# Output projection of the first layer begun inside the last head pair

## The chip, the cores and the metric

The kernel runs on one core of a Trainium2 chip. The metric is the time of one launch in device microseconds (us), as the median of several runs. All times below are microseconds unless marked ns. Engines: PE is the tensor engine (PEld its weight loads), DVE the vector engine, ACT the scalar engine, POOL the GpSimd engine, SP the sync engine, which here issues nearly all DMAs. Each engine runs its instructions in program order.

## The reference, cut to what matters

Two layers of a trunk run over 640 tokens (512 latent tokens and 128 prompt tokens) of width 1024. In the first layer twelve RWKV-7 heads give 768 features and a Fourier mixer gives 256; one output projection joins them, and a mixture of 16 experts follows.

```
h = rmsnorm(x, norm_mix[l]) * (1 + sc1) + sh1
...
o_a, s_fin = rwkv7_mixer(h, r, k, v, ...)      # 12 heads of 64
o_b = fourier_mixer(u)                          # 256 features
mixed = concatenate([o_a, o_b]) @ ev_w_out      # (640 x 1024) @ (1024 x 1024)
x = x + gt1 * mixed
h2 = rmsnorm(x, norm_ffn[l]) * (1 + sc2) + sh2
x = x + gt2 * expert_choice_ffn(h2, ...)        # 16 experts, 80 token rows each
```

Each head's result is normalised over its 64 features, scaled, shifted, given a bonus and multiplied by a gate before it enters the projection.

## The kernel before

Activations lie transposed: a tile is 128 features (partitions) by 640 tokens. A 128x1024 slice of the features is one of eight *chunks*; `mix[:, c]` holds the input chunks of the projection. Products into PSUM are written to a *pair* of banks, `pair(q)`, as 512 columns and 128 columns. All matmuls named here are float32, and the profile shows two records for each of them.

The program is a row of stages. A stage (`with stage() as block`) holds one instruction stream for each engine, and no engine begins the next stage before all have ended this one (the *border*). `even_heads()` is one stage: six head pairs, the last of them by `heads(False)` on PE and ACT and `heads(HP - 1, False)` on DVE. Its end for the last pair is a chain: PE forms y in `pair(3)`; ACT copies it (L1136, `y_sbuf`); PE forms the mean in `pair(2)` (L982); DVE subtracts it (L1294); ACT squares (L1144); PE forms the variance in `pair(1)` (`y_variance`, L794); ACT takes the root (L1076); DVE takes the reciprocal in four parts (L1302), scales, shifts, adds the bonus and gates into `mix[:, 0]` (L1320). Earlier pairs lie in `mix[:, 1]` to `mix[:, 5]`, written while the pair after them is worked on, and the Fourier part lies in `mix[:, 6:8]` from the opening. So of the eight input chunks of the projection only one, `mix[:, 0]`, comes from this chain.

`out_proj` is the next stage. SP issues four transfers of 1 MB with the output weights (L1462, into the start of the work area, where `mat` of the heads lay) and after the first of them the reload of `x` from device memory (L1464, 2.5 MB; the heads use the memory of `x` as work space). PE goes over eight output tiles m; each is eight chunks for the 512 columns and then eight for the 128 columns (L1475), in `pair(m % 3)`, and from the fourth tile on it waits for DVE to have read an earlier one (`out_read`). DVE adds each tile, times a modulation, to `x` (L1496). ACT squares `x` (`square_x`, L126), and PE sums the squares in two halves (`sum_x`, L133), the second after the last tile. Then ACT copies the sums (L142) and PE turns them (`turn_sums`, L148).

The stage after it is `norm_route(0, ...)`: filler matmuls (`keep_busy`, L154, products of the identity that nothing reads), `token_rates` on DVE (L231), `spread_rates` on PE (L237), the scaled h, the router and a top-k on DVE. Then `experts(0)`: the weights of the experts come in slabs of 2 MB through `RAW` = 4 slots; ACT rounds each piece (a quarter of a slab, 128x1024) to a high part (`high`, L1814), DVE forms the low part (`low`, L1872), and PE takes six matmuls a piece (L1747). `SPLIT` = 8 buffers stand between them. At the beginning ACT and DVE each make `AHEAD` = 7 pieces before they turn to the token rows: PE runs 20 fillers and turns the fetched rows (L1756), ACT takes their high part (L1819), DVE their low part (L1868), and then PE begins with the pieces. One round of the loop is 48 pieces, eight rounds a layer. `experts` and `norm_route` are used for both layers.

SP's stream in `even_heads` loads weights, vectors and state of the pair to come. `win` (the input weights of a pair, at `PAIR0[0]` of the work area) is free once the last projections of the coming pair are made, of which `icl_tanh(1)` on ACT tells (`win_free`).

## Time and profile before

| what | value |
|---|---|
| runs | 2649.55, 2640.97, 2643.34; median 2643.34 |
| profiled execution | 2638.59, span of its instructions 2636.7 |
| PE busy, share of the span | 91% |
| DVE, ACT, POOL | 68%, 48%, 6% |
| mean granted clock of PE | 0.966 of full speed |
| last pair's end, from the mean to the gated chunk | 969.9 to 985.9 |
| output projection, first to last matmul | 991.3 to 1065.0 |
| expert stages begin their pieces | 1126.7 and 2042.8 |

Times within the profile count from the start of the span. The clock is given as a share of full speed; it has two levels, 0.50 (1.2 GHz) and 1.00 (2.4 GHz). A window whose clock lies between had both.

### The profile page before, as it was taken

The page shows a single profiled execution, that of the slowest core. Times are in us where ns is not written, and L with a number is a line of the kernel's source. Part 1 is how long each engine was busy: PE and PEld are TensorE (multiplying, and loading weights), DVE is VectorE, ACT ScalarE, POOL GpSimd, SP SyncE. Part 2 cuts the span into 40 slices and gives each one's busy share as a digit, 9 for nine tenths or more (in the row PEclk, how much of TensorE's full clock was granted, in tenths as well). Part 3 has the DMA queues.
Part 4 walks back from the last instruction along what each step waited for, and adds up shares of the span by engine and source line. Part 5 has one row for each costly group of instructions (what it writes and reads, how often), then busy time and mean ns, then how long its engine had stood idle before and what let it go on. Part 6 is the DMA issues. An engine that isn't in the chain of part 4 may idle for free. (4 is left out here: it accounts for less than half of the span.)

```text
span 2636.7 us, 51914 instructions
## 1 busy us (share of the span) xinstructions
PE 2386.4 (91%) x19628; PEld 1596.0 (61%) x19628; DVE 1801.4 (68%) x2293; ACT 1255.1 (48%) x1545; POOL 154.5 (6%) x160
## 2 busy tenths in 40 slices
PE   5977999999999769699999999889896999999997
PEld 2435767677676655466666666645454666666665
DVE  2317565657565620589999999469615999999994
ACT  2012323232323210377878888410303887788883
POOL 1000000000000000000000000000000000000000
PEclk8988999999999989799999999999997999999999
DMA  9950010101010002499999999421005999999993
GB/s 365 393 219 28 3 30 4 30 3 30 3 31 3 4 7 99 182 358 378 386 381 388 383 385 386 136 115 50 15 1 205 374 389 383 388 385 386 383 387 106
DMA packets 176368, 539.35 MB, mean 205 GB/s; under 512 B 12417, under 2 KB 48897, under 8 KB 176066
## 3 DMA queue, kind: packets, MB, share of 16 engines
q1 hardware_dynamic: 169666, 514.63, 50.8%
q0 software_dynamic: 6528, 22.29, 3.6%
q8 instruction: 122, 2.00, 0.3%
q14 instruction: 52, 0.43, 0.1%
HBM read 510.29 MB, written 26.61 MB: 204 GB/s over the span
## 5 line engine op out<-in xcount | busy, mean ns | idle before, releaser
L1872 DVE TENSOR_TENSOR wl<-raw,wh 128x1024 fp32r<-128x1024 f32 x768 | 897.9, 1221 | 82.3 <-DVEq L1871 74.9
L1814 ACT ACTIVATE wh<-raw 128x1024 fp32r<-128x1024 f32 x768 | 796.3, 1057 | 240.1 <-ACTq L1813 228.6
L1747 PE MATMUL ps<-wh,xs 128*80 128x512 f32 x3072 | 845.2, 393 | 5.8 <-PEq L1742 5.8
L1747 PEld LDWEIGHTS ps<-wh,xs 128*80 128x80 f32 x3072 | 449.7, 148 | 244.7 <-issue 6.7
L1747 PE MATMUL ps<-wl,xs 128*80 128x512 f32 x1536 | 476.6, 391 | 0.0
L1747 PEld LDWEIGHTS ps<-wl,xs 128*80 128x80 f32 x1536 | 227.5, 148 | 127.3 <-issue 0.7
L1372 DVE COPY_PREDICATED wk<-m,ps 128x512 f32<-128x512 uint8 x180 | 131.1, 732 | 109.4 <-DVEq L1371 108.5
L739 PE MATMUL ps<-h,wk 128*128 128x512 f32 (+1 forms) x576 | 176.5, 448 | 3.9 <-PEq L987 2.7
L1096 ACT ACTIVATE wk<-ps 128x256 f32<-128x256 f32 (+1 forms) x180 | 65.6, 365 | 201.8 <-ACTq L1095 201.8
L739 PEld LDWEIGHTS ps<-h,wk 128*128 128x128 f32 x576 | 93.8, 192 | 77.6 <-issue 74.1
L126 ACT ACTIVATE h<-x 128x640 f32<-128x640 f32 x40 | 28.5, 733 | 208.4 <-ACTq L123 146.8
L1991 PE MATMUL ps<-h,wk 128*128 128x512 f32 (+1 forms) x448 | 122.0, 434 | 3.3 <-PEq L1982 3.3
L154 PE MATMUL ps<-cst 128*128 128x128 f32 x706 | 107.8, 303 | 12.2 <-PEq L1802 5.8
L865 PE MATMUL ps<-wk 64*64 64x64 f32 x2400 | 107.3, 224 | 8.8 <-issue 6.1
L882 PE MATMUL ps<-wk 64*64 64x64 f32 x2400 | 100.4, 219 | 11.3 <-issue 11.3
L869 PE MATMUL ps<-wk 64*64 64x64 f32 x2400 | 103.1, 221 | 5.0 <-issue 4.9
L154 PEld LDWEIGHTS ps<-cst 128*128 128x128 f32 x706 | 94.4, 210 | 17.9 <-issue 14.5
L1991 PEld LDWEIGHTS ps<-h,wk 128*128 128x128 f32 x448 | 68.0, 191 | 57.0 <-issue 57.0
L1724 POOL DMA_INDIRECT ysum<-rows,idx x32 | 50.8, 1588 | 789.9 <-POOLq L1722 789.9
L2241 DVE SCALAR_TENSOR_TENSOR wk<-wk 128x670 f32<-128x670 f32 x116 | 96.4, 910 | 0.4 <-DVEq L2235 0.4
L865 PEld LDWEIGHTS ps<-wk 64*64 64x64 f32 x2400 | 85.9, 133 | 14.4 <-issue 9.9
L882 PEld LDWEIGHTS ps<-wk 64*64 64x64 f32 x2400 | 86.2, 135 | 13.1 <-issue 12.9
(283 smaller groups left out, 2749.9 us busy)
## 6 DMA issues: line engine op xcount, KB each, us to landing
raw<-in_moe_w_gate SPq DMA_DIRECT2D x64, 2048.0 KB, 10.5
raw<-in_moe_w_up SPq DMA_DIRECT2D x64, 2048.0 KB, 11.4
raw<-in_moe_w_down SPq DMA_DIRECT2D x64, 2048.0 KB, 11.5
wk<-in_mod_w SPq DMA_DIRECT2D x24, 2048.0 KB, 11.3
wk<-in_ev_w_in SPq DMA_DIRECT2D x18, 512.0 KB, 4.9
wk<-in_od_w_in SPq DMA_DIRECT2D x4, 2048.0 KB, 15.7
ysum<-raw SPq DMA_DIRECT2D x10, 512.0 KB, 16.4
hrow<-rows SPq DMA_DIRECT2D x10, 512.0 KB, 4.9
```

Source lines behind the costliest of these rows:

```text
L154: pe.matmul(ps[:, bank, 0:P], ident, ident, start=True, stop=True)
L739: last = pe.matmul(pair(q)[:, a:b], win[:, c, s], h[:, c, a:b], start=c == 0, stop=c == KC - 1)
L865: pe.matmul(ps[to:te, zb, slotT(z, hh):slotT(z, hh) + HD], lhs, rhs, start=True, stop=True)
L869: last = pe.matmul(ps[to:te, zb + 1, slotN(z, hh):slotN(z, hh) + HD], lhs, rhs, start=True, stop=True)
L882: last = pe.matmul(ps[to:te, 2 + u % 2, at:at + HD], mat[lo:hi, g, z, hh, 0, lo:hi], inv(g, z, hh, lo, hi), start=True, stop=True)
L1096: act.activation(yw[:, g].rearrange("p z h n -> p (z h n)")[:, 0:w], ps[:, 2 + u % 2, 0:w], ACT.Copy).then_inc(sem("yw_copied"), 1)
L1372: dve.copy_predicated(xx[:, g].rearrange("p z k h n -> p z k (h n)"), bcast(lv[:, q // NT], 2, 2), ps[:, zbank(q):zbank(q) + 2, 0:4 * HD]. ...
L1747: last = pe.matmul(ps[0:CAP, b0 + k], lhs[:, xk, c, :], w[:, s, a:b], start=c == 0 and xk == 0 and w is wh, stop=c == KC - 1 and xk == 1)
L1814: act.activation(wh[:, n % SPLIT], raw[:, n // 4 % RAW, n % 4], ACT.Copy).then_inc(sem("high_ready"), 1)
L1872: dve.tensor_tensor(wl[:, n % SPLIT], raw[:, n // 4 % RAW, n % 4], wh[:, n % SPLIT].bitcast(F32), ALU.subtract).then_inc(sem("low_ready"), 1)
L1991: last = pe.matmul(place(q)[:, a:b], win[:, m // 4, c, m % 4 * P:(m % 4 + 1) * P], h[:, c, a:b], start=c == 0, stop=c == KC - 1)
L2241: dve.scalar_tensor_tensor(to, src, cw[:, c, k:k + 1], to, ALU.mult, ALU.add).then_inc(sem("tap"), 1)
```

## The change

The output weights are loaded in the stage of the heads: the first quarter into the place of `win` once that is free, the other three into the place of `mat` once ACT has copied y of the last pair (`mat_free`). After the variance of the last pair PE computes output tiles 0 and 1 over the seven chunks that are ready (`EARLY_OUT`), in `pair(3)` and `pair(2)`, and leaves both sums open; the eighth chunk follows in the next stage. Chunks are now the outer loop, the two column parts the inner one. The pairs of the tiles follow `OUT_AT`, and PE waits for readers from tile 4 on. The stage of the projection has only the reload of `x` left for SP. Six fillers stand before the second half of the sum of squares. In both expert stages `AHEAD` is 4 for 7, and 18 fillers stand for 20. `ymean_read` is now signalled in the last pair too.

```diff
--- before.py
+++ after.py
@@ -199,7 +199,7 @@
                 work.clear()
 
         PIECES = 48
-        RAW, SPLIT, AHEAD = 4, 8, 7
+        RAW, SPLIT, AHEAD = 4, 8, 4
 
         @contextmanager
         def expert_memory(layer):
@@ -617,6 +617,26 @@
                     for l, n in ((0, 1), (1, 0), (1, 1)):
                         take_gain(l, n)
 
+
+        def out_weights():
+
+            late = Carve()(3, KC, 256)
+            return [Carve(PAIR0[0])(KC, 256)] + [late[:, q] for q in range(3)]
+
+        def load_out(sp, q, w):
+
+            sp.dma_start(out_weights()[q], w[:, q * 256:(q + 1) * 256].rearrange("(c p) n -> p c n", p=P)).then_inc(sem(f"slab{q}"), 16)
+
+        OUT_AT = (3, 2, 0, 1, 2, 0, 1, 2)
+
+        def out_chunk(pe, m, c, first, last):
+
+            mix = work["mix"]
+            for a, b in ((0, NS), (NS, T)):
+                mm = pe.matmul(pair(OUT_AT[m])[:, a:b], out_weights()[m // 2][:, c, m % 2 * P:(m % 2 + 1) * P], mix[:, (c + 1) % HP if c < HP else c, a:b], start=first, stop=last)
+            return mm
+
+        EARLY_OUT = [c for c in range(KC) if c != HP - 1]
 
         def even_heads():
             mix, lora, wk = work["mix"], work["lora"], work["area"]
@@ -716,9 +736,13 @@
                         load_gate(i + 1)
                     sp.wait_ge(sem("hpv_free"), 1).then_inc(sem("hpv_free"), -1)
                     sp.wait_ge(sem("win_free"), 1).then_inc(sem("win_free"), -1)
+                    load_out(sp, 0, t["ev_w_out"])
                     sp.wait_ge(sem("state_free"), 1).then_inc(sem("state_free"), -1)
                     sp.wait_ge(sem("sout_ready"), 1).then_inc(sem("sout_ready"), -1)
                     sp.dma_start(outv[HP - 1], sout).then_inc(sem("state_out"), 16)
+                    sp.wait_ge(sem("mat_free"), 1).then_inc(sem("mat_free"), -1)
+                    for q in range(1, 4):
+                        load_out(sp, q, t["ev_w_out"])
                     sp.wait_ge(sem("wg_free"), 1).then_inc(sem("wg_free"), -1)
                     sp.wait_ge(sem("state_out"), 16).then_inc(sem("state_out"), -16)
 
@@ -983,6 +1007,12 @@
                         last.then_inc(sem("ymean_ready"), 1)
                         if not following:
                             y_variance()
+                            pe.wait_ge(sem("slab0"), 16).then_inc(sem("slab0"), -16)
+                            for c in EARLY_OUT:
+                                out_chunk(pe, 0, c, c == 0, False)
+                            pe.wait_ge(sem("ymean_read"), 1).then_inc(sem("ymean_read"), -1)
+                            for c in EARLY_OUT:
+                                out_chunk(pe, 1, c, c == 0, False)
 
                     pe.wait_ge(sem("slab4"), 64).then_inc(sem("slab4"), -64)
                     project(K, 0, range(KC))
@@ -1134,7 +1164,7 @@
                             act.wait_ge(sem("ahead_done"), 1).then_inc(sem("ahead_done"), -1)
                         act.wait_ge(sem("y_ready"), 1).then_inc(sem("y_ready"), -1)
                         act.activation(ysb, pair(3), ACT.Copy).then_inc(act_done, 1)
-                        done("y_sbuf")
+                        done("y_sbuf", *(() if following else ("mat_free",)))
                         if following:
                             copy_gate("gate_read")
                             copy_bonus()
@@ -1423,9 +1453,8 @@
                             dve.wait_ge(sem("ar_read"), 1).then_inc(sem("ar_read"), -1)
                             queries()
                         y_centred()
-                        if following:
-                            dve.sem_inc(sem("ymean_read"), 1)
-                        else:
+                        dve.sem_inc(sem("ymean_read"), 1)
+                        if not following:
                             for k in range(4):
                                 y_rate(k)
                             y_scaled()
@@ -1450,34 +1479,30 @@
                     heads(HP - 1, False)
 
 
-        def out_proj(l, w):
-            cv = Carve()
-            w_sb = cv(4, KC, 256)
-            mix = work["mix"]
+        def out_proj(l):
 
             with stage() as block:
                 @block.sync
                 def _(sp):
-                    for q in range(4):
-                        sp.dma_start(w_sb[:, q], w[:, q * 256:(q + 1) * 256].rearrange("(c p) n -> p c n", p=P)).then_inc(sem(f"wout{q}"), 16)
-                        if q == 0:
-                            sp.dma_start(x[:, :, :], t["xsave"].rearrange("(c p) n -> p c n", p=P)).then_inc(sem("x_back"), 16)
+                    sp.dma_start(x[:, :, :], t["xsave"].rearrange("(c p) n -> p c n", p=P)).then_inc(sem("x_back"), 16)
 
                 @block.tensor
                 def _(pe):
                     for m in range(KC):
-                        if m % 2 == 0:
-                            pe.wait_ge(sem(f"wout{m // 2}"), 16).then_inc(sem(f"wout{m // 2}"), -16)
-                        if m >= 3:
-                            pe.wait_ge(sem("out_read"), 1).then_inc(sem("out_read"), -1)
-                        for a, b in ((0, NS), (NS, T)):
+                        if m < 2:
+                            last = out_chunk(pe, m, HP - 1, False, True)
+                        else:
+                            if m % 2 == 0:
+                                pe.wait_ge(sem(f"slab{m // 2}"), 16).then_inc(sem(f"slab{m // 2}"), -16)
+                            if m >= 4:
+                                pe.wait_ge(sem("out_read"), 2 if m == 4 else 1).then_inc(sem("out_read"), -2 if m == 4 else -1)
                             for c in range(KC):
-                                last = pe.matmul(pair(m % 3)[:, a:b], w_sb[:, m // 2, c, m % 2 * P:(m % 2 + 1) * P], mix[:, (c + 1) % HP if c < HP else c, a:b],
-                                                start=c == 0, stop=c == KC - 1)
+                                last = out_chunk(pe, m, c, c == 0, c == KC - 1)
                         last.then_inc(sem("out_ready"), 1)
                         if m == KC - 2:
                             sum_x(pe, 0)
                     pe.wait_ge(sem("out_read"), 3).then_inc(sem("out_read"), -3)
+                    keep_busy(pe, 0, 6)
                     sum_x(pe, 1)
                     turn_sums(pe)
 
@@ -1493,7 +1518,7 @@
                     for m in range(KC):
                         dve.wait_ge(sem("out_ready"), 1).then_inc(sem("out_ready"), -1)
                         for r, a, b in SEGS:
-                            dve.scalar_tensor_tensor(x[:, m, a:b], pair(m % 3)[:, a:b], mod[:, l, 2, m, r:r + 1], x[:, m, a:b], ALU.mult, ALU.add).then_inc(dve_done, 1)
+                            dve.scalar_tensor_tensor(x[:, m, a:b], pair(OUT_AT[m])[:, a:b], mod[:, l, 2, m, r:r + 1], x[:, m, a:b], ALU.mult, ALU.add).then_inc(dve_done, 1)
                         dve.wait_ge(dve_done, 2).then_inc(dve_done, -2)
                         dve.sem_inc(sem("out_read"), 1)
                         dve.sem_inc(sem("x_ready"), 1)
@@ -1762,7 +1787,7 @@
                         turn(4 * ee, xtok[:, ee]).then_inc(sem("xs_turned"), 1)
 
                     pe.sem_inc(sem("split_free"), SPLIT - 1)
-                    keep_busy(pe, 7, 20)
+                    keep_busy(pe, 7, 18)
                     turn_xs(0)
                     with pe.Fori(0, E // 2) as i:
                         for n in range(PIECES):
@@ -2324,7 +2349,7 @@
         with mixer_memory(0):
             opening()
             even_heads()
-            out_proj(0, t["ev_w_out"])
+            out_proj(0)
         with expert_memory(0):
             norm_route(0, fill(0))
             experts(0)
```

## Rows read from the trace of the kernel before

**Rows 1.** The page, costliest groups: busy, mean ns | idle before, releaser.

```profile
L1747 PE MATMUL ps<-wh,xs 128*80 128x512 f32 x3072 | 845.2, 393 | 5.8 <-PEq L1742 5.8
```

**Rows 2.** Timeline, end of the last pair: start, length, engine, line, operation, idle before.

```profile
973.44 2.47 PE L794 MATMUL ps<-wk,cst 128*128 128x512 f32 x4 [2.26 <-PEq L792]
...
977.11 5.05 DVE L1302 RECIPROCAL x<-x 128x160 f32<-128x160 f32 x4 [4.94 <-DVEq L1301]
...
985.12 0.82 DVE L1320 TENSOR_TENSOR mix<-x 128x640 f32<-128x640 f32 x1 [0.26 <-DVEq L1319]
...
991.29 9.11 PE L1475 MATMUL ps<-mix,wk 128*128 128x512 f32 x14 [15.37 <-PEq L1470]
```

**Rows 3.** Windows: busy of PE, PEld, DVE, ACT, POOL; then clock, DMA share, GB/s.

```profile
973.40:976.00 2.60, 2.47 (x4) 1.18 (x4) 0.00 (x0) 0.00 (x0) 0.00 (x0) 0.50 0.00 0
...
991.20:997.00 5.80, 5.71 (x7) 2.50 (x8) 0.00 (x0) 0.00 (x0) 0.00 (x0) 0.50 1.03 406
997.00:1065.10 68.10, 68.02 (x266) 37.75 (x264) 7.06 (x14) 4.93 (x7) 0.00 (x0) 1.00 0.13 47
...
1068.80:1072.30 3.50, 2.27 (x11) 2.24 (x11) 0.00 (x0) 0.72 (x2) 0.04 (x1) 0.50 0.00 0
```

**Rows 4.** Timeline: two chunks with chunks outermost, and tiles of the projection.

```profile
307.79 2.43 PE L739 MATMUL ps<-h,wk 128*128 128x512 f32 x8
...
1020.50 1.01 DVE L1496 SCALAR_TENSOR_TENSOR x<-ps,mod,x 128x512 f32<-128x512 f32 x2 [7.64 <-DVEq L1494]
...
1029.15 1.01 DVE L1496 SCALAR_TENSOR_TENSOR x<-ps,mod,x 128x512 f32<-128x512 f32 x2 [7.65 <-DVEq L1494]
...
1056.10 8.92 PE L1475 MATMUL ps<-mix,wk 128*128 128x512 f32 x32
```

**Rows 5.** SP in the last pair, and DMA issues by size and time to landing.

```profile
862.65 0.35 SPq L695 DMA_DIRECT2D wk<-in_lora  x1
...
wk<-in_ev_w_out SPq DMA_DIRECT2D x4, 1024.0 KB, 12.3
...
x<-xsave SPq DMA_DIRECT2D x1, 2560.0 KB, 11.1
```

**Rows 6.** Timeline, end of the projection and beginning of the routing stage.

```profile
1065.17 1.01 DVE L1496 SCALAR_TENSOR_TENSOR x<-ps,mod,x 128x512 f32<-128x512 f32 x2 [9.05 <-DVEq L1494]
...
1067.43 1.28 PE L133 MATMUL ps<-h,mean 128*32 128x512 f32 x16 [2.41 <-PEq L130]
...
1069.73 2.27 PE L148 MATMUL ps<-cst,h 128*128 128x1 f32 x10 [1.02 <-PEq L146]
...
1072.30 2.47 PE L154 MATMUL ps<-cst 128*128 128x128 f32 x10 [0.30 <-PEq L94]
...
1072.97 0.15 DVE L231 RECIPROCAL tokstat<-tokstat 128x5 f32<-128x5 f32 x1
...
1074.56 1.76 PE L237 MATMUL ps<-cst,tokstat 128*128 128x128 f32 x10
```

**Rows 7.** Timeline, beginning of the first expert stage.

```profile
1116.33 6.42 PE L154 MATMUL ps<-cst 128*128 128x128 f32 x40 [0.98 <-PEq L94]
...
1117.61 8.04 DVE L1872 TENSOR_TENSOR wl<-raw,wh 128x1024 fp32r<-128x1024 f32 x7 [1.86 <-DVEq L1871]
...
1123.51 0.70 ACT L1819 ACTIVATE xs<-ps 128x640 fp32r<-128x640 f32 x1 [0.37 <-ACTq L1817]
...
...
1126.67 1.04 PE L1747 MATMUL ps<-wh,xs 128*80 128x512 f32 x2 [3.37 <-PEq L1742]
```

**Rows 8.** Timeline, beginning of the second expert stage.

```profile
2033.76 8.04 DVE L1872 TENSOR_TENSOR wl<-raw,wh 128x1024 fp32r<-128x1024 f32 x7 [1.86 <-DVEq L1871]
...
2040.63 0.70 ACT L1819 ACTIVATE xs<-ps 128x640 fp32r<-128x640 f32 x1 [1.34 <-ACTq L1817]
...
2042.82 0.67 PE L1747 MATMUL ps<-wh,xs 128*80 128x512 f32 x2 [2.40 <-PEq L1742]
```

**Rows 9.** Windows over the matmuls of one round of experts: busy, clock, DMA share, GB/s.

```profile
1197.30:1263.60 66.30, 64.49 (x280) 40.68 (x278) 1.00 1.02 389
```

## The prediction

> **What bounds the kernel now.** I read the page first. The costliest group is the expert matmuls, and PE stood idle before them for only 5.8 us in all [rows 1]: over both expert stages PE sets the time, and whatever brings their beginning forward brings the end of the kernel forward by as much. Between them lie chains in which one engine waits for another. So I read the timeline from the last head pair to the first expert piece.
>
> There the reader sees PE finish the variance at 973.44 + 2.47 = 975.91 and stand idle for 15.37 us until 991.29 [rows 2]. In this gap ACT takes a root, DVE works from 977.11 (four reciprocals, 5.05 in all) to the gated chunk at 985.12 + 0.82 = 985.94, the border passes, and the first weights land. The windows show that PE runs the variance at clock 0.50, and the first 5.7 us of the projection too, before it comes to 1.00 for the rest [rows 3]. From then on PE is full: an output tile every 1029.15 - 1020.50 = 8.65 us, DVE idle 7.6 of them, and the last matmul ends at 1056.10 + 8.92 = 1065.02 [rows 4]. So two things bound this stretch, PE's own work of 8 x 8.65 = 69.2 and the 15.37 in which it could not start.
>
> **Early tiles.** Only one chunk of eight comes from DVE's chain; the seven others are written long before. The change puts 2 x 7 chunks behind the variance. One chunk, both column parts, costs 8.65 / 8 = 1.08 at full clock, so this is 15.1 us of PE work. With chunks outermost two chunks took 2.43 in another projection of this kernel [rows 4]; that length includes the end of the last matmul, so 1.22 a chunk is the upper bound and 1.08 the value I take, as the records are the same in number and shape. The upper bound would add 64 x 0.14 = 9 us in all; the row's own tail makes it unlikely, and I keep it outside the likeliest case.
>
> The weights for them must be there. SP's last act for the coming pair is the load at 862.65 [rows 5]; the two semaphores it then waits for are signalled in the same stretch, so the first quarter is asked for some 110 us before PE needs it, against a landing time of 12.3 [rows 5]. What it is moved past on SP is only the wait for the state and its output. The three other quarters are issued when ACT has copied y, which the mean at 969.9 had to wait for, so some 6 us before the variance ends; SP then issues nothing else in this stage but the wait for the gate weights, long free. In the old order four such loads, with the reload of x among them, took a median of 12.3 to land [rows 5], so these are there by about 983, before PE wants the second quarter at about 995. Cost nothing; the cover is the early tiles.
>
> The clock: before, PE ran at 0.50 in the variance, then idle. Now it does not pause. The clock rose after 5.7 us of work in [rows 3]; if so here, it rises at 973.44 + 5.7 = 979.1, and 3.2 us of early work at half speed cost 1.6. The other end is that it rises as the variance ends and costs 0. I take 1.2, nearer the row. The slow start at 991.29, worth 5.7 / 2 = 2.9, is gone.
>
> Sum for PE: 975.91 + 1.2 + 15.1 = 992.2, which is 6.3 after DVE's chunk, so PE is now last at the border and the DVE chain is hidden. The border cost PE 0.30 at the next stage [rows 6]: 992.5. Two last chunks, 2.2: 994.7. Six tiles, 51.9: 1046.6. First half of the sum of squares between the tiles, 1.28 (as [rows 6] has the second): 1047.9. Before it was 1065.02. **Gain 17.1**, bounds 16.7 and 18.3.
>
> **The reload of x** moves later, from 986.8 to about 992.5, but it now has the DMA to itself. Beside the weights it took 11.1 [rows 5]: landed by 1003.6. DVE then takes tiles 0 and 1 by 1005.7, while tile 4, the first for which PE waits for readers, would begin at 994.7 + 17.3 = 1012. Over 6 us to spare; DVE needs 1.01 a tile of 8.65 and has caught up by then. Cost nothing. `ymean_read`, the other new wait of PE, is signalled by DVE before the variance; nothing is held up behind it.
>
> **End of the projection.** DVE ends tile 7 1.16 after PE's last matmul, and PE used to begin its sum 2.41 after it, when ACT's square was done [rows 6]. Now six fillers (12 records) stand before it, and they can only begin when DVE is done. Ten records took 2.47 at clock 0.50 [rows 6], so 12 take 1.5 at 1.00: PE begins at 1065.02 + 1.16 + 0.2 + 1.5 = 1067.9 on the old scale, 0.5 later than before. What they may bring is the clock: behind the gap of 2.41 it fell to 0.50, and the turning of the sums (2.27), the fillers (2.47) and the spreading of the rates (1.76) ran slow, wholly or in part [rows 3, 6]. The rates were ready at 1072.97 + 0.15 = 1073.12, but spreading began at 1074.56, behind the fillers. At full clock the first saves 1.1, the second 1.2, the third some 0.2, and the rates are still ready before the fillers end. **Gain 2.0**, bounds -0.5 (it falls all the same) and 2.2. I take 2.0, since the pauses that are left, 1.4 and 1.0, are shorter than the 2.41 before the fall.
>
> The Trainium skill, page "TensorE: Matmul & The Clock Gate", Part 1, says that the chip's look at activity runs free of the kernel, so that the matmul at which the clock changes differs from run to run. By that rule both clock terms could fall differently in each execution; the two terms would then scatter between my bounds, which are 1.6 and 2.7 us apart. The trace of one execution cannot show whether it holds here.
>
> **Expert stages.** In the first, DVE made seven low parts until 1117.61 + 8.04 = 1125.65, while ACT had the high part of the rows at 1124.21; PE began at 1126.67, about 1.0 after DVE's lows ended [rows 7]. With four, DVE is done at 1117.61 + 4.6 = 1122.2 and waits for ACT instead. PE turned the rows right behind its fillers; four records fewer of 0.16 bring ACT forward by 0.5, to 1123.7. DVE's part costs 0.82 (as in the old spacing, 1.0 from its start to PE), with a handover of 0.3: PE begins at 1125.1, gain 1.6. In the second stage the lows ended at 2041.80 and ACT at 2041.33 [rows 8]; with ACT at 2040.8 PE begins at about 2042.2 for 2042.82, gain 0.6. Does the smaller lead starve PE? DVE makes a piece in 8.04 / 7 = 1.15, PE takes 66.3 / 48 = 1.38 [rows 7, 9], so the missing 3 pieces are never wanted: DVE has the fifth ready 2.6 after PE starts, and PE wants it after 5.5. **Gain 2.2**, bounds 0 and 3.9 (if the shorter wait also keeps the clock, which was full in the second stage behind a wait of 2.40 and fell before the first piece behind 3.37 [rows 7, 8], 1.7 more).
>
> **Sum.** 17.1 + 2.0 + 2.2 = 21.3. The profiled execution took 2638.6 (span 2636.7), so it becomes 2617.3. The median of the runs stands 4.7 above it, at 2643.3: **2622.0**.
>
> **The rivals**, each with the time it gives.
> - *The clock falls at the projection's end all the same* (15%). The fillers then cost 0.5 and bring nothing: 2643.3 - 18.8 = 2624.5. For it speaks that pauses of 1.4 and 1.0 remain close together.
> - *The weight stream sets the expert loop* (7%). It moved 389 GB/s with a DMA share of 1.02 [rows 9]; were it the limit, an earlier start of PE would be lost in the loop: 2643.3 - 19.1 = 2624.2. Against it speak the 5.8 us of [rows 1]. The Trainium skill, page "DMA: Bandwidth & Descriptors", section Bandwidth, holds that HBM gives one core about 358 GB/s; by that rule the loop would be bound by the stream and this rival true, but the trace shows 389.
> - *PE stays at 0.50 through the early tiles* (5%). They cost 15.1 more for my 1.2: gain 7.4, 2635.9. Against it: the clock rose within 5.7 us of work in [rows 3].
> - *The change doesn't do what it says* (3%): something holds the early chunks back behind DVE's chain, so that only the loads are hidden. PE starts at 986.3 for 991.29, 5.0, plus the other terms 4.2: 2634.1.
> - *The clock is kept at the first expert stage too* (5%): 2620.3.
> - *The other side: the expert loop lives on its lead* (2%). If three pieces of lead were never rebuilt, PE would wait up to 3 x 1.38 = 4.1 at each of the two places in a round where DVE leaves the pieces for the hidden layer, 32 places: 132 us against 19.1 gained, 2756. It decides from 0.9 us a place on. Against it: DVE gains 0.23 on PE with every piece, so it has the lead back in 18.
> - The rest, 63%, is the forecast.
>
> **How the numbers follow.** A measurement of this kernel can tell about 0.3%, 8 us. All cases but three give more than that; PE slow throughout gives 7.4, just inside, and with part of the blocked case and scatter I put 5% within 0.3%, 3% slower, 92% faster. The range: from below, 2622.0 less 1.2 (clock early), 1.7 (clock at the experts) and the 2.4 between the lowest run and the median gives 2616.7, widened to 2615 for fewer slow stretches elsewhere; from above, the two rivals together 2626.7 and the 6.2 by which the highest run lies over the median give 2632.9. So 2615 to 2633; the three cases outside hold 10%.
>
> **What would show it.** In the changed profile: PE busy from the variance to the border, the first early chunk right behind it, and 2 x 7 chunks ending 6 us after DVE's gated chunk; the last matmul of the projection some 17 earlier; clock 1.00 in the turning of the sums and in the fillers of the next stage; PE beginning the pieces 1.6 and 0.6 sooner after the fillers' start (8.8 for 10.3 in the first stage) with no new idle before them. Wrong would be: a wait of PE for the first quarter or for readers at tile 4, a chunk at 1.2 for 1.08, or idle time before the expert matmuls well above 5.8 us.

## The result

The changed kernel took 2612.78 us (median of 4 runs, 2607.94 to 2622.64); the kernel before, run beside it, 2646.45 (4 runs, 2640.97 to 2651.15). The ratio is 0.9878, with an interval of [0.984, 0.9917] that lies below 1: faster, by 1.2%. The forecast was 2622.0 with a range of 2615 to 2633, so direction and rough size are right and the median lies 2.2 below the range. The profiled execution took 2616.19, with a span of 2614.4, against a forecast of 2617.3 for it.

From the page of the changed kernel; the last row answers to [rows 1]:

```profile
PE 2391.9 (91%) x19632; PEld 1602.4 (61%) x19632; DVE 1801.2 (69%) x2293; ACT 1255.9 (48%) x1545; POOL 155.0 (6%) x160
...
L1772 PE MATMUL ps<-wh,xs 128*80 128x512 f32 x3072 | 843.8, 393 | 4.6 <-PEq L1767 4.6
```

PE still sets the time of the expert stages: 4.6 idle for 5.8, so no new wait came in. (The 3072 records of this row are one for each matmul: two layers of 8 x 48 pieces with four products of `wh` each. What the opening says of two records a matmul holds for the other matmuls named there, not for these.) The timeline of the changed kernel from the variance to the scaled h answers to [rows 2, 4, 6]:

```profile
967.85 2.47 PE L818 MATMUL ps<-wk,cst 128*128 128x512 f32 x4 [2.26 <-PEq L816]
...
970.11 15.82 PE L636 MATMUL ps<-mix,wk 128*128 128x512 f32 x56
...
979.52 0.82 DVE L1350 TENSOR_TENSOR mix<-x 128x640 f32<-128x640 f32 x1 [0.26 <-DVEq L1349]
...
986.19 0.37 SPq L1487 DMA_DIRECT2D x<-xsave  x1
...
996.64 1.01 DVE L1521 SCALAR_TENSOR_TENSOR x<-ps,mod,x 128x512 f32<-128x512 f32 x2 [16.30 <-DVEq L1519]
...
1033.04 8.92 PE L636 MATMUL ps<-mix,wk 128*128 128x512 f32 x32
...
1043.42 1.58 PE L154 MATMUL ps<-cst 128*128 128x128 f32 x12 [1.46 <-PEq L1504]
1044.92 1.28 PE L133 MATMUL ps<-h,mean 128*32 128x512 f32 x16
1047.23 1.25 PE L148 MATMUL ps<-cst,h 128*128 128x1 f32 x10 [1.03 <-PEq L146]
1048.78 1.67 PE L154 MATMUL ps<-cst 128*128 128x128 f32 x10 [0.30 <-PEq L94]
1050.24 2.34 PE L237 MATMUL ps<-cst,tokstat 128*128 128x128 f32 x10
...
1052.73 0.69 DVE L249 TENSOR_TENSOR h<-x,ps 128x512 f32<-128x512 f32 x1 [3.13 <-DVEq L242]
```

The 15.37 of idle time is gone: the first early chunk begins at 970.11, where the variance ends, and 14 chunks end at 970.11 + 15.82 = 985.93. DVE's gated chunk is done at 979.52 + 0.82 = 980.34, 5.6 sooner. The last matmul of the projection ends at 1033.04 + 8.92 = 1041.96, 74.11 after the variance begins, where it was 1065.02 - 973.44 = 91.58. The reload of x landed 10.2 after its issue (DVE's first tile is at 996.64) and held nobody. Behind the last matmul the second sum starts at 1044.92, 2.96 later for 2.41 before; the turning runs in 1.25 for 2.27, but the spreading takes 2.34 for 1.76.

The windows of the changed kernel give the granted clock (the column behind POOL), to be read beside [rows 3]; they are the variance, the early chunks, the turning, and the fillers with the spreading:

```profile
967.80:970.30 2.50, 2.45 (x5) 1.45 (x6) 0.00 (x0) 0.00 (x0) 0.00 (x0) 0.50 1.08 384
970.30:985.90 15.60, 15.60 (x57) 8.47 (x55) 7.70 (x8) 0.79 (x1) 0.00 (x0) 0.97 0.26 92
1047.20:1048.70 1.50, 1.25 (x10) 1.19 (x10) 0.00 (x0) 0.00 (x0) 0.00 (x0) 1.00 0.00 0
1048.80:1052.60 3.80, 3.80 (x22) 3.80 (x23) 0.65 (x2) 0.22 (x1) 1.55 (x5) 0.61 0.65 107
```

The clock is full almost from the first early chunk on (0.97 over all of them), is kept in the turning, and falls behind it, which the forecast did not expect.

The beginning of the first expert stage in the changed kernel answers to [rows 7]:

```profile
1099.90 0.70 ACT L1844 ACTIVATE xs<-ps 128x640 fp32r<-128x640 f32 x1 [3.38 <-ACTq L1842]
...
1100.75 0.82 DVE L1893 TENSOR_TENSOR xs<-ps,xs 128x640 fp32r<-128x640 f32 x1 [2.29 <-DVEq L1892]
...
1101.87 0.65 PE L1772 MATMUL ps<-wh,xs 128*80 128x512 f32 x2 [2.17 <-PEq L1767]
```

DVE now waits 2.29 for ACT instead of the other way round. PE's first piece begins 9.31 after the fillers start at 1092.56, for 10.34 before, and its first two records take 0.65.

### The profile page after: what moved, and what is told of

The parts are those of the page before. It is cut to its first block and busy times, and to the rows that moved or that the text cites. A ratio compares the mean times of both kernels' runs of the same rounds, so it can differ in the third digit from the quotient of the medians.

```text
span 2614.4 us, 51925 instructions
## 1 busy us (share of the span) xinstructions
PE 2391.9 (91%) x19632; PEld 1602.4 (61%) x19632; DVE 1801.2 (69%) x2293; ACT 1255.9 (48%) x1545; POOL 155.0 (6%) x160
## 5 line engine op out<-in xcount | busy, mean ns | idle before, releaser
L126 ACT ACTIVATE h<-x 128x640 f32<-128x640 f32 x40 | 28.5, 733 | 189.8 <-ACTq L123 129.6
## 6 DMA issues: line engine op xcount, KB each, us to landing
wk<-in_od_w_in SPq DMA_DIRECT2D x4, 2048.0 KB, 15.1
```

## The experiments

What differs between executions is large against some of the terms, so the trace is read by distances between marks that the change touches: from the start of the last variance to the last matmul of the projection; from there to the scaled h; and from the fillers of an expert stage to the end of its loop of pieces, taken where the fillers behind the loop begin. Before, in the profile shown, these were 91.58, 11.45, 563.20 and (second layer) 561.41; after, 74.11, 10.77, 560.28 and 560.04. Where no diff is shown, the kernel is the changed one.

**The same kernel again**, twice, in other comparisons.

> The changed kernel once more, beside the kernel before on one chip. Theory 1: the two profiles differ by 22.2 in the places that the change touches (17.5 to the last matmul of the projection, 0.7 to the first scaled h, 2.9 in the first expert stage, 1.1 in the second), and the rest of the 33.7 between the first medians is scatter of single executions (opening, clock elsewhere). Then 22 less than before here, between 17 and 27. Theory 2: the change is worth about 32, and 10 of it did not show between the two profiles. Then 29 to 35 less.

> The changed kernel a third time, on this call's chip, to narrow its time. The first comparison gave a ratio of 0.988, the second 0.991. If the local terms are all (22 of 2645), 0.9915; if the change is worth 32, 0.988. From the variance's start to the first scaled h 84.9 as in both profiles so far, or 83.4 when the variance runs at full clock.

Measured: 2620.01 (8 runs, 2605.35 to 2629.88), ratio 0.9914 [0.9883, 0.9945]; and 2618.95 (9 runs, 2612.77 to 2633.65), ratio 0.9904 [0.9876, 0.9933]. The marks of the projection repeat closely: 74.17 and 74.18 to the last matmul, 10.72 and 10.66 to h. The total does not: with the first comparison there are 21 runs with a median of 2618.95 and a standard deviation of 8.1, between 2605.35 and 2633.65. So the change is worth 22.8 of 2647 by the ratio in the first of the two and 27.0 by the medians, nearer theory 1 than theory 2, and 25.4 by the ratio in the second, between them. The 49 runs of the kernel before in the same comparisons have a median of 2647.8, a deviation of 8.3, and lie between 2637.23 and 2673.61.

**One part alone.** First the early tiles and loads without the change in the expert stages; then the kernel before with only that.

```diff
# e2_projection_only, against the changed kernel
-RAW, SPLIT, AHEAD = 4, 8, 4
+RAW, SPLIT, AHEAD = 4, 8, 7
-keep_busy(pe, 7, 18)
+keep_busy(pe, 7, 20)
# e3_experts_only: the kernel before, with 4 for 7 and 18 for 20
```

> The changed kernel with AHEAD 7 and 20 fillers again in the expert stages, so the projection's part alone. Theory 1: 4 more than the changed kernel, so 18 less than before. Theory 2 with its 10 in the expert stages: 14 more than the changed kernel; theory 2 with its 10 in the projection: 28 less than before.

> The kernel before with AHEAD 4 and 18 fillers, nothing else. Theory 1: 4 less than before (1.6 and 0.6 by the waits, 1.7 for the clock at the first stage when it is kept). Theory 2 with its 10 in the expert stages: 12 to 14 less. If the weight stream set the loop: 0. If the smaller lead starved PE: more than before.

Measured, each over 12 runs: 2626.36, ratio 0.9935 [0.991, 0.996], and 2637.5, ratio 0.9986 [0.9958, 1.0014]. Of 2647 these are 17.2 and 3.7; together 20.9, beside the 0.0086 x 2647 = 22.8 of the whole change in the same comparison. The sum fits, but the totals alone don't prove it: the second interval holds 1, and the medians themselves differ from 2646.97 by 20.6 and 9.5. The marks say where: with the projection alone 72.49 to the last matmul, and loops of 562.80 and 563.19, as before; with the experts alone 90.09, and loops of 560.38 and 560.00. The 72.49 and 90.09 differ from 74.11 and 91.58 because the last variance ran in 1.32 and 1.77 in these executions; the edit doesn't touch that. The shorter lead is worth some 2 to 3 in the first loop and 1 to 3 in the second.

**Loads early, tiles late.** The weights come early but PE computes nothing before the border.

```diff
# e4_tiles_late
-for c in EARLY_OUT:
-    out_chunk(pe, 0, c, c == 0, False)
...
-for c in EARLY_OUT:
-    out_chunk(pe, 1, c, c == 0, False)
...
-    last = out_chunk(pe, m, HP - 1, False, True)
+    for c in range(KC):
+        last = out_chunk(pe, m, c, c == 0, c == KC - 1)
```

> The changed kernel with the loads early, but no early tiles: all eight chunks of every tile in the projection's stage. Theory 1: the projection starts 5.0 sooner than before in place of 17.5, at the low clock again, and the other parts give 4.7: 10 less than before. The profile should show PE idle for some 10 us after the variance and tile 0 at clock 0.50. If the early tiles were worth nothing, it would equal the changed kernel.

Measured: 2635.06 (12 runs), ratio 0.9947 [0.9913, 0.998]. PE's timeline in this kernel:

```profile
979.40 2.07 PE L818 MATMUL ps<-wk,cst 128*128 128x512 f32 x4 [2.25 <-PEq L816]
991.92 8.52 PE L636 MATMUL ps<-mix,wk 128*128 128x512 f32 x21 [10.46 <-PEq L94]
```

PE is idle for 10.46 behind the variance, then starts 12.52 after its beginning for 17.85: the loads alone are worth 5.3 at the start and 91.58 - 85.84 = 5.7 to the last matmul, 0.4 of it from a variance of 2.07 for 2.47. The early tiles bring the rest of the 17.5, about 11.7: they fill the wait for DVE, and they spare the slow start, which is back here (clock 0.50 from 991.9 to 996.0, 0.78 in the 2 us after).

**The fillers before the second sum**: taken out, and made more.

```diff
# e5_no_fill
-keep_busy(pe, 0, 6)
 sum_x(pe, 1)
 turn_sums(pe)
# e6_turn_filled
 keep_busy(pe, 0, 6)
 sum_x(pe, 1)
+keep_busy(pe, 0, 4)
 turn_sums(pe)
+keep_busy(pe, 0, 2)
```

> The changed kernel without the six fillers before the second half of the sum of squares. Theory 1 (the fillers hold the clock and cost 0.5): that sum starts 2.4 behind the last matmul in place of 3.0, then the turning of the sums takes 2.3 in place of 1.25, and the first scaled h comes 11.5 behind the last matmul as before the change, in place of 10.8. Rival (the clock is set by where the stretch falls, not by the fillers): the turning stays at 1.25, and h comes 10.2 behind.

> The changed kernel with four more fillers between the second sum and the turning of the sums, and two behind it. In the profiles of the changed kernel the clock held through the turning and fell just behind it, so that the spreading of the rates took 2.34 each time. Theory 1 (the fall answers to the idle and one-column stretch from 1046 to 1049): with fillers there the spreading takes 1.25 and h comes 9.7 behind the last matmul for 10.8. Rival (it falls there anyway): 2.34 again, and h 11.0 behind.

PE in the kernel without fillers:

```profile
1051.79 1.28 PE L133 MATMUL ps<-h,mean 128*32 128x512 f32 x16 [2.41 <-PEq L130]
1054.09 2.08 PE L148 MATMUL ps<-cst,h 128*128 128x1 f32 x10 [1.02 <-PEq L146]
1056.46 2.47 PE L154 MATMUL ps<-cst 128*128 128x128 f32 x10 [0.30 <-PEq L94]
1058.73 2.34 PE L237 MATMUL ps<-cst,tokstat 128*128 128x128 f32 x10
```

and in the kernel with more:

```profile
1047.09 1.15 PE L154 MATMUL ps<-cst 128*128 128x128 f32 x8
1048.08 1.17 PE L148 MATMUL ps<-cst,h 128*128 128x1 f32 x10
1049.11 0.69 PE L154 MATMUL ps<-cst 128*128 128x128 f32 x4
1050.10 1.35 PE L154 MATMUL ps<-cst 128*128 128x128 f32 x10 [0.30 <-PEq L94]
1051.29 1.28 PE L237 MATMUL ps<-cst,tokstat 128*128 128x128 f32 x10
```

Without fillers h comes 11.84 after the last matmul, with those of the change 10.77, with more 9.98. The turning is a train of products with one column, with a pause of 1.03 ahead of it. In the kernel with fillers on both sides of it the clock stays, the following fillers take 1.35 for 1.67 and the spreading 1.28 for 2.34. One execution each: 2616.89 and 2609.85. The totals can't tell a microsecond, the marks can.

That the added fillers are what keeps the clock is not shown by this alone. The kernel of the next experiment (e7) has nothing around its turning, as the changed kernel, and kept the clock too:

```profile
1046.71 1.35 PE L154 MATMUL ps<-cst 128*128 128x128 f32 x10 [0.30 <-PEq L94]
1047.90 1.28 PE L237 MATMUL ps<-cst,tokstat 128*128 128x128 f32 x10
```

Without the cost of more fillers, h came 9.44 behind the last matmul there. Over all profiles the clock was kept in both kernels with fillers around the turning (e6 and e11 below), and in one of the eight with six fillers before the second sum and none around the turning; in the other seven it fell behind the turning. The count speaks for the fillers, but the rival, that the fall depends on where the stretch comes in the execution, has a part.

**Chunks before the variance.** PE waits 2.26 ahead of the variance. Two early chunks go there.

```diff
# e7_chunks_sooner
+pe.wait_ge(sem("slab0"), 16).then_inc(sem("slab0"), -16)
+for c in EARLY_OUT[:2]:
+    out_chunk(pe, 0, c, c == 0, False)
 y_variance()
-pe.wait_ge(sem("slab0"), 16).then_inc(sem("slab0"), -16)
-for c in EARLY_OUT:
+for c in EARLY_OUT[2:]:
     out_chunk(pe, 0, c, c == 0, False)
```

> The changed kernel with the first two early chunks before the variance in place of behind it, where PE waits 2.26 for ACT's square. Theory 1: they hide in that wait, and the clock is not lost before the variance, so the variance takes 1.3 in place of 2.5 and the rest is fast from its first chunk: 2.2 + 1.2 + 0.5 less than the changed kernel, from the start of the mean to the last matmul. Rival (the chunks delay the variance and with it DVE's chain): nothing lost either as PE is last at the border by 5, unless the variance starts more than 5 late.

PE in this kernel:

```profile
967.15 2.33 PE L636 MATMUL ps<-mix,wk 128*128 128x512 f32 x8
969.57 1.32 PE L818 MATMUL ps<-wk,cst 128*128 128x512 f32 x4
970.73 13.14 PE L636 MATMUL ps<-mix,wk 128*128 128x512 f32 x48
984.17 45.67 PE L636 MATMUL ps<-mix,wk 128*128 128x512 f32 x168 [0.30 <-PEq L94]
```

The two chunks fill the wait and the variance runs in 1.32 for 2.47. The last matmul comes 70.33 after the variance begins for 74.11: 3.8, for a forecast of 3.9. The variance is not delayed, it begins 3.56 after the mean in both. The total: 2611.78 (6 runs), ratio 0.9877 [0.9844, 0.991].

**More early work.** Tile 0 replaces the fillers in the four steps of the last pair, tile 1 lies around the variance, tile 2 behind it.

```diff
# e8_in_steps
-OUT_AT = (3, 2, 0, 1, 2, 0, 1, 2)
+OUT_AT = (1, 3, 0, 2, 1, 0, 2, 1)
...
-keep_busy(pe, 5, 3)              # in step j of the last pair
+out_chunk(pe, 0, EARLY_OUT[2 * j], j == 0, False)
...
-keep_busy(pe, 5, 5)
+out_chunk(pe, 0, EARLY_OUT[2 * j + 1], False, False)
...
+for c in EARLY_OUT[:2]:
+    out_chunk(pe, 1, c, c == 0, False)
+y_variance(2)
+for c in EARLY_OUT[2:]:
+    out_chunk(pe, 1, c, c == 0, False)
+for c in EARLY_OUT:
+    out_chunk(pe, 2, c, c == 0, False)
```

> Three early tiles: the seven ready chunks of tile 0 stand in the place of the fillers of the last pair's steps, two of tile 1 before the variance, five behind it, then seven of tile 2. Theory 1 (PE's own work sets the time from the variance on, so each chunk moved before it is worth 1.08): 7.5 for tile 0 and 3.9 as with the sooner chunks: 10 to 11 less than the changed kernel, less 1 if the chunks delay the steps. Now DVE's gated chunk, 12.5 behind the start of the variance, and PE's 12 chunks behind it are about even. Rival (the steps wait for PE and each chunk delays them by its length over the fillers'): the heads grow by up to 2, and 8 to 9 remain.

PE in two of the steps:

```profile
930.47 1.30 PE L636 MATMUL ps<-mix,wk 128*128 128x512 f32 x4
...
938.98 2.45 PE L636 MATMUL ps<-mix,wk 128*128 128x512 f32 x4
```

From the first step of the last pair (L965) to the last matmul it takes 104.31 for the 112.08 of the change: 7.8 less, not the 10 to 11 of theory 1. The steps themselves grew by 2.1, half of it where the clock fell in one step and the chunk took 2.45 for 1.30. A new wait cost another 1.2: the reload of x, issued at 983.33, lets DVE begin its first tile at 993.96, and PE at tile 4 waits until DVE has read tile 1:

```profile
993.96 1.01 DVE L1530 SCALAR_TENSOR_TENSOR x<-ps,mod,x 128x512 f32<-128x512 f32 x2 [13.83 <-DVEq L1528]
...
996.72 3.48 PE L636 MATMUL ps<-mix,wk 128*128 128x512 f32 x12 [1.20 <-PEq L1507]
```

So with three early tiles the reload, which cost nothing in the change, comes onto the path. Total 2609.43 (6 runs), ratio 0.9888 [0.9846, 0.9929], an interval that overlaps those of the change: here too only the marks tell.

**A lead of one piece.** If the lead fed PE, one piece would show it.

```diff
# e9_lead_one
-RAW, SPLIT, AHEAD = 4, 8, 4
+RAW, SPLIT, AHEAD = 4, 8, 1
```

> The changed kernel with AHEAD 1 for 4, so that one piece lies ready when PE begins. My theory: DVE and ACT make a piece in 1.15 to 1.23 and PE takes 1.38, so the lead comes back; from the fillers' start to the end of the expert loop 560 to 562 as with 4 (560.3). Rival (the expert loop lives on its lead, and DVE's longer works for the hidden layer make PE wait when it is short): more than 564, growing with the 16 such places in the first rounds.

The loops took 561.14 and 561.67 for 560.28 and 560.04 in the changed kernel, and PE's idle time before the pieces was 4.3. So DVE does rebuild the lead, even from six pieces fewer than before; the rival on the other side, which priced three fewer at 132, falls. The total, 2629.05 in one execution, comes from the heads, which took 807.22 there for 796.00.

**All that was found**: e8 with the fillers of e6.

> The kernel with early chunks in the steps of the last pair, and with the fillers around the turning of the sums. By the local terms: 7.8 less than the changed kernel to the last matmul of the projection, counted from the last pair's first step, and 0.8 to 1.0 less from there to the first scaled h: 9 less in all, 31 less than before, ratio 0.988. The spreading of the rates takes 1.28. Rival (the clock is lost elsewhere for it): 2.34 there and 8 less.

Measured: 2605.07 (6 runs, 2601.02 to 2617.82), ratio 0.9834 [0.9801, 0.9867], the lowest median here, though its interval still overlaps those of e7 and e8. From the first step of the last pair to h it takes 112.46, for 122.85 in the changed kernel: 10.4, where 9 was forecast; the spreading takes 1.28. Its interval lies below those of the two repeats of the change ([0.9876, 0.9933] in the same comparison, 2618.95 for 2605.07) and overlaps that of the first; together with the marks this makes it faster than the change.

**The kernel before, profiled again**, three times, with nothing changed: how far do executions of one kernel differ, and where?

> The kernel before, unchanged, profiled again. All runs so far give 28.5 less for the change (plus or minus 4.3), the marks of the first profiles 22.4. If the profile shown first is like the others of its kernel: from the variance's start to the first scaled h 103.0, from the fillers to the end of the expert loop 563.2 and 561.4. If it was a favourable one: up to 5 more in one of these, which names the place of the remainder.

> As the run before it: a further profile of the unchanged kernel before, to see how its marks scatter. Marks alike: the remainder lies outside the places that the change touches. Marks higher by 2 to 5: it lies in them.

> A third profile of the unchanged kernel before, for the scatter of its marks; expectations as for the two before it.

They took 2662.58, 2641.96 and 2640.41. The first against the one of the forecast, over the heads up to the last variance and over one slice of 50 us (windows of each; the first column after the window's bounds is its length, the share behind POOL the clock). First the slow one:

```profile
177.26:995.36 818.10, 731.91 (x11757) 558.66 (x11757) 482.29 (x834) 234.60 (x462) 44.05 (x62) 0.95 0.05 14
677.30:727.30 50.00, 47.29 (x480) 35.23 (x475) 21.23 (x54) 15.52 (x34) 3.12 (x6) 0.76 0.01 3
```

then the kernel before as the forecast had it:

```profile
177.37:973.44 796.07, 710.22 (x11756) 543.65 (x11757) 482.27 (x834) 234.25 (x462) 44.06 (x62) 0.98 0.05 14
677.30:727.30 50.00, 47.52 (x311) 34.53 (x308) 27.95 (x60) 18.65 (x34) 3.13 (x6) 1.00 0.01 3
```

DVE has the same 482.3 of work in the heads in both; PE has 21.7 more busy time at a clock of 0.95 for 0.98, and the heads take 22.0 longer: two of the pairs took 138.6 and 136.4 from one variance to the next, for 126.4 and 126.0. So one stage can move two executions of one kernel apart by as much as the whole change gives.

The marks of the profile shown first were not favourable ones: from the variance to h 103.03, with 101.62, 101.74 and 103.11 in the other three, and loops of 563.20 and 561.41, with 562.8 and 562.8, 562.9 and 561.5, 562.7 and 563.0. The remainder is not in the places that the change touches.

## Why the prediction was right, and where it failed

**What bounds the kernel**: right. The gap behind the variance was idle time of PE on the path, and what was filled came back at the end of the kernel.

**Early tiles, forecast 17.1**: right. The distance from the variance to the last matmul fell by 91.58 - 74.11 = 17.5, and by 16.8 over all profiles of the two kernels (90.95 and 74.15). The 14 chunks took 15.82, or 1.13 each with the tail of the last and what was left of the slow clock in it, so nearer 1.08 than 1.22; the border cost 0.30; the early tiles end 5.6 behind DVE's chunk for 6.3. The clock penalty of 1.2 was too high: 15.82 less 15.1 leaves at most 0.7 for it, and 0.97 over the early chunks (15.6 x 0.03) says 0.5.

**Loads and reload, forecast nothing**: right. The first quarter was issued at 858.05, the other three at 964.30, with no wait of PE; x came in 10.2.

**End of the projection, forecast 2.0**: the mechanism was right and the size wrong. It measured 0.7. The 0.5 that the fillers cost was right (2.96 for 2.41), and so was the clock kept in the turning (1.0 saved). The step that failed is "at full clock the second saves 1.2, the third some 0.2". The clock fell behind the turning, the next fillers kept part of their 2.47 (1.67), and the spreading lost 0.6. My reason, that the pauses of 1.4 and 1.0 are shorter than the 2.41 before the fall, looked at the pauses alone; what decides the fall is not settled (e6 kept the clock with fillers around the turning, e7 without them). The rival "the clock falls all the same", 15%, was half true. Nor is the stretch of before always the same: in e3, whose code up to h is that of before, the clock fell in the second sum already (2.03 for 1.28) and h came 12.76 behind the last matmul, for 11.38 to 11.45 in the four profiles of before.

**Expert stages, forecast 1.6 + 0.6 = 2.2**: measured 2.9 and 1.4. The handover in the first stage gave 1.0, not 1.6. DVE's wait for ACT is right, and the hops behind ACT too (0.15 to DVE, 0.82 and 0.30 to PE). What failed is "four records fewer of 0.16 bring ACT forward by 0.5". The windows of PE over the fillers and the turning of the rows, and over the wait and the first pieces, in the changed kernel:

```profile
1092.60:1094.60 2.00, 2.00 (x9) 0.50 0.04 8
1094.60:1096.60 2.00, 2.00 (x12) 0.50 0.68 170
1096.60:1099.00 2.40, 2.40 (x20) 0.83 0.47 131
1099.00:1103.00 4.00, 1.83 (x15) 1.00 0.67 224
```

and in the kernel before, where the last is the first pieces alone:

```profile
1116.40:1118.40 2.00, 2.00 (x10) 0.50 0.04 8
1118.40:1120.40 2.00, 2.00 (x13) 0.62 0.69 168
1120.40:1122.80 2.40, 2.40 (x26) 1.00 0.44 133
1126.70:1128.70 2.00, 2.00 (x5) 0.52 1.02 420
```

The clock rose later in the fillers, so 36 records took 6.59 where 40 had taken 6.42, and ACT got its rows no sooner. What made up for it is the bound to which I gave 5%: behind a wait of 2.17 for 3.37 the clock is kept (1.00 for 0.52), and the end of the loop comes 2.9 sooner, not 1.0. This repeats in every profile: in all eleven of a kernel with a lead of 4 or 1 and 18 fillers the clock is 1.00 over the first 8 us of the pieces in both stages, and in all five with a lead of 7 (the four of before and e2) it is down at the first pieces of the first stage. In three of these five it falls at the second stage too, though not in the profile that the forecast read:

```profile
2064.01:2068.00 3.99, 3.99 (x12) 2.41 (x13) 2.20 (x2) 2.12 (x2) 0.00 (x0) 0.67 1.05 380
```

(e12, from its first piece of the second stage), and in the changed kernel:

```profile
2020.70:2024.70 4.00, 4.00 (x23) 2.81 (x24) 4.00 (x4) 4.00 (x5) 0.00 (x0) 1.00 1.05 394
```

So the kept clock belongs in the sum at both stages, and a single profile hid it at the second. A lead of 4 starves nothing, as e9 with a lead of 1 shows more strongly. The weight stream doesn't set the loop: in e3 PE starts 1.06 earlier and the loop ends 2.8 earlier.

The Trainium skill, page "DMA: Bandwidth & Descriptors", section Bandwidth, gives about 358 GB/s as the HBM limit of one core, and by that figure the earlier start would have been lost in the loop. The same section has 425 GB/s for a core whose neighbour is idle, which the prediction passed over. The trace shows 389 [rows 9], above the first figure and below the second, and the loop ended earlier by more than PE started earlier.

**The sum.** Over all profiles of the two kernels (four of before, three of after), from the variance to h: 102.4 and 84.9, 17.5 less; the two loops with their starts 562.9 and 560.6, 562.2 and 560.8, that is 2.3 and 1.4 less. Together 21.2, for a forecast of 21.3. The terms' errors, -0.3 for the early tiles, -1.3 for the projection's end and +1.5 for the experts, cancel: that the sum is right to 0.1 is luck.

**The range, where it was wrong.** The measured median lies 9.2 below the forecast of 2622.0 and outside the range. Of the 9.2, the sum of gains has only 1.1: the profiled execution took 2616.19 for 2617.3. The other 8.1 are in one term, "the median of the runs stands 4.7 above it": in these four runs the median stood 3.4 below the profiled execution. Such a term says where one execution happens to lie among others of its kernel; the change has no part in it, and the range should have held it. Its lower end was worked out as 2622.0 less 1.2, less 1.7, and "the 2.4 between the lowest run and the median", for the scatter of runs. That step failed: the scatter was sized far too small. Three runs of one kernel showed 8.6 between them; 21 runs of the changed one show 28.3, with a deviation of 8.1. A median of four scatters by about 1.25 x 8.1 / 2 = 5.1, so an error of 10 is within twice that (an estimate from these runs). The first one was 2612.78 where the two repeated ones were 2620.0 and 2619.0. Those two lie inside the range, and within about 3 of the forecast. Over the 21 runs the median, 2618.95, stands 2.8 to 6.2 above the three profiled ones, so the 4.7 was a fair value that four runs could not show. The Trainium skill, page "TensorE: Matmul & The Clock Gate", Part 1, which I weighed against the clock terms only, says that the look at activity runs free of the kernel, so that results change from run to run. The traces agree that they do, and in the heads as well, which I did not cost: the variance of before took 2.47, 1.32, 1.32 and 2.47 in its four profiles, and the heads 796.07 to 818.10. That this is the reason no run here shows.

**What stays open.** All 21 runs against all 49 differ by 28.5, with 2 x the root of 8.1²/21 + 8.3²/49, that is 4.3, to either side; the marks give 21.2. By the ratios of the three comparisons, 1.22%, 0.86% and 0.96%, weighted by their runs, it is 0.97% or 25.7. The remaining 4.5 to 7.3 lie outside the places that the change touches. In the first pair of profiles the opening ends 5.5 earlier (heads from 171.85 for 177.37), while the work between the loops of the two layers took 358.62 for 352.95, with the clock at 0.70 and 0.61 in two windows of 5 where before it was full:

```profile
1860.00:1865.00 5.00, 5.00 (x24) 0.70 0.00 0
1865.00:1870.00 5.00, 5.00 (x13) 0.61 0.00 0
```

The first is not seen in the other two profiles of the changed kernel (174.69 and 175.62) to that size, nor the second (354.21 and 352.90). The heads up to the last variance took 801.3 on average in five profiles with the old loads (794.55 to 818.10) and 796.3 in nine with the new ones (790.43 to 807.22). I can't tell chance from a small effect there; no run separated them.

## What to carry over

Cost a change by distances between marks of the trace near the edit: in three profiles of the changed kernel they repeat to 0.1 us in the projection and to 1.2 in the loops, where totals scatter by 8. Where the clock differs between executions a mark moves too (by 1.3 to 1.7 with the last variance), so read the clock beside it, and in more than one profile where you can. Make the range from the scatter of totals: with three runs, whose spread says little, ask which long stage has a clock that is not full throughout, and let the range take in what that can move (here 22 in a stage of 800). When an engine waits for a chain of others, look for sums that can be begun with the operands that are ready: they fill the wait and keep the clock for what follows.

## What the hardware showed that I had not expected

- Behind the turning, ten records with one column and a pause of 1.03 ahead, the clock fell in seven of eight profiles although it was full during the turning (1.00, then 0.61 over the next 3.8, in the first); with eight filler records ahead of it and four behind, the spreading took 1.28 for 2.34 in both profiles, but once also without them.
- Before the first expert piece PE waited 2.17 to 2.45 in both stages of the eleven profiles with the short lead, and the clock stayed full. With a lead of 7 it waited 3.06 to 3.47 in the first stage, and the clock fell in all five; in the second it stayed full behind 2.40 and 2.75 and fell behind 2.81, 2.88 and 3.54. From the first piece to the loop's end that stage took 551.1 in the two where the clock stayed and 552.4 to 552.8 in the three where it fell. The length of the wait does not decide alone: at the end of the projection before, the clock fell behind 2.41.
- The same place runs at either level in executions of one kernel: the last variance of the kernel before took 2.47, 1.32, 1.32 and 2.47. In the first profile of the changed kernel the clock rose within 1 us of its end; in [rows 3] it rose 5.7 into the projection.
- Two executions of one kernel differed by 22.0 in the stage of the heads alone, with 21.7 more of PE's busy time at a clock of 0.95 for 0.98.
- The reload of x (2.5 MB) landed in 10.2 alone for 11.1 with 4 MB beside it: having the DMA to itself brought this transfer 0.9 in one execution of each.
